# A hybrid encoder layer on one core: the first projection taken by halves of the rows for both column groups, with the input's halves loaded on ScalarE's queue

## The reference

```python
proj = x @ w_in
hq, hf, hi, hg, cq, ckv, su, lx, lg, gl = jnp.split(proj, IN_OFFSETS, axis=-1)
y_a = hgrn2_mixer(hq, hf, hi, hg, lb, hgrn_norm_w)
y_b = mla_mixer(cq, ckv, positions, ...)
y_c = s5_mixer(su, s5_a_re, s5_a_im, s5_log_dt, ...)
y_d = rglru_mixer(lx, lg, lru_conv_w, lru_conv_b, lru_wa, ...)
...
mix = jnp.sum(gates * branch_out, axis=2) @ w_out
h = layer_norm(DEEPNORM_ALPHA * x + mix, ln1_w, ln1_b)
ffn = moe_ffn(h, router_w, router_b, moe_w1, moe_b1, moe_w2, moe_b2)
return layer_norm(DEEPNORM_ALPHA * h + ffn, ln2_w, ln2_b)
```

```python
xc = lax.conv_general_dilated(x_raw, conv_w..., padding=[(LRU_CONV - 1, 0)], ...) + conv_b
r = jax.nn.sigmoid(jnp.einsum('bshi,hij->bshj', xb, wa)... + ba)
i = jax.nn.sigmoid(jnp.einsum('bshi,hij->bshj', xb, wx)... + bx)
```

## Time and profile before

| what | value |
|---|---|
| median of the timed runs | 1310.3 us (1309.55 to 1311.1) |
| the profiled execution's own time | 1309.58 us |
| its span | 1307.8 us |
| TensorE busy | 1251.4 us, 96% |
| VectorE / ScalarE busy | 455.6 us (35%) / 219.9 us (17%) |
| DMA, mean over the span | 351 GB/s, 458.99 MB |
| DMA, 460 to 1290 us | 428 to 431 GB/s |

### The profile page before, as it was taken

One profiled execution on the slowest core, in us unless ns is written; L12 is line 12 of the kernel. 1 busy time (PEld: TensorE's weight loads), 2 busy tenths in 40 slices (PEclk: granted clock), 3 DMA queues, 4 the chain that ended last, 5 costly groups with the idle time before them and its releaser, 6 DMA issues.

```text
span 1307.8 us, 15059 instructions
## 1 busy us (share of the span) xinstructions
PE 1251.4 (96%) x6094; PEld 637.9 (49%) x6094; DVE 455.6 (35%) x919; ACT 219.9 (17%) x430; POOL 4.0 (0%) x20
## 2 busy tenths in 40 slices
PE   9999999999999999999999999989999998999996
PEld 8888888998753333333333333333333333333331
DVE  4679965365347122121221212132121212132123
ACT  1432224131031101101011010101101010101102
POOL 0000000000000000000000000000000000000000
PEclk9999999999999999999999999999999999999998
DMA  9434344226788999999999999999999999999995
GB/s 366 164 144 142 113 146 161 99 95 229 277 346 363 396 432 431 432 431 432 432 431 428 431 430 431 432 430 430 429 429 430 430 431 432 432 432 426 426 424 237
DMA packets 29132, 458.99 MB, mean 351 GB/s; under 512 B 4464, under 2 KB 4848, under 8 KB 9104
## 3 DMA queue, kind: packets, MB, share of 16 engines
q1 hardware_dynamic: 25936, 454.04, 83.1%
q10 hardware_dynamic: 3136, 4.03, 0.9%
HBM read 457.02 MB, written 1.05 MB: 350 GB/s over the span
## 4 chain that ended last, share of the span: by engine, by line
PE 61%; DMA 22%; DVE 13%; ACT 2%; issue 1%; SPq 0%; DVEq 0%; ACTq 0%
DMA store<-in_moe_w 21%; PE banks L1208 16%; PE banks L1238 12%; PE banks L810 11%; PE banks L824 4%; PE banks L1214 3%; DVE store L1879 2%; PE banks L1090 2%; PE banks L1295 2%; PE banks L1140 2%; DVE store L1873 1%; DVE store L1876 1%; DVE store L1878 1%; ACT store L707 1%; PE banks L1224 1%
## 5 line engine op out<-in xcount | busy, mean ns | idle before, releaser
L1208 PE MATMUL banks<-store 128*64 128x512 f32 x1536 | 344.3, 597 | 23.5 <-DMA store<-in_moe_w 20.7
L1208 PEld LDWEIGHTS banks<-store 128*64 128x64 f32 x1536 | 111.0, 137 | 239.9 <-issue 210.4
L1238 PE MATMUL banks<-store 128*64 128x512 f32 x960 | 213.1, 596 | 0.0
L810 PE MATMUL banks<-store 128*128 128x256 f32 x896 | 196.4, 380 | 0.0
L810 PEld LDWEIGHTS banks<-store 128*128 128x128 f32 x896 | 169.5, 190 | 25.7 <-issue 3.0
L1873 DVE TENSOR_SCALAR store<-banks 128x512 f32<-128x512 f32 x32 | 22.1, 692 | 439.7 <-PE banks L1214 439.7
L1238 PEld LDWEIGHTS banks<-store 128*64 128x64 f32 x960 | 66.4, 137 | 145.4 <-issue 121.9
L1214 PE MATMUL banks<-store 128*64 128x512 f32 x512 | 116.9, 598 | 0.3 <-DMA store<-in_moe_w 0.3
L707 ACT ACTIVATE store<-store 128x512 f32<-128x512 f32 x30 | 19.0, 632 | 453.8 <-DVE store L1873 453.8
L1887 DVE COPY store<-banks 64x512 f32<-64x512 f32 x30 | 20.8, 694 | 206.8 <-PE banks L1238 206.8
L1140 PEld LDWEIGHTS banks<-store 128*128 128x128 f32 x480 | 57.0, 191 | 25.1 <-issue 23.5
(11 more groups left out here) (374 smaller groups left out, 837.9 us busy)
## 6 DMA issues: line engine op xcount, KB each, us to landing
store<-in_moe_w SPq DMA_DIRECT2D x78, 4096.0 KB, 35.3
store<-in_moe_w SPq DMA_DIRECT2D x32, 2048.0 KB, 16.1
store<-in_w_in SPq DMA_DIRECT2D x30, 1024.0 KB, 4.8
store<-in_w_branch SPq DMA_DIRECT2D x8, 1024.0 KB, 4.8
store<-in_moe_w SPq DMA_DIRECT2D x8, 1024.0 KB, 37.4
store<-in_w_out SPq DMA_DIRECT2D x4, 1024.0 KB, 6.8
store<-in_xT SPq DMA_DIRECT2D x2, 512.0 KB, 5.9
store<-in_w_in SPq DMA_DIRECT2D x2, 512.0 KB, 7.4
```

The costliest lines, as they stand in the source:

```text
L810: last = mm(b[:, j * SEQ:(j + 1) * SEQ], w[:, k, j * P:j * P + P], xT[:, k, :], start=k == 0, stop=k == KD - 1)
L1208: last = mm(bank[i][64 * ct:64 * ct + 64, :], xg[:, 2 * c + kk, col:col + CAP], w[:, kk, i * FF + ct * 512:i * FF + ct * 512 + 512], start ...
L1238: last = mm(bank[4][64 * dh:64 * dh + 64, :], actT[:, j, 64 * fh:64 * fh + 64], w[:, j, 512 * dh:512 * dh + 512], start=(fh, j) == (0, 0), ...
```

## The change

The two loads of `xT` move from SP to ScalarE, where they stand ahead of everything. SP keeps the two loads of the first chunk and goes straight on with the others. TensorE no longer finishes group 0 before group 1: it takes row blocks 0 to 3 for both groups when `first_in[0]` is full, then row blocks 4 to 7 for both groups when `first_in[1]` is. As both sums are then open at once, group 1 goes into bank 2 in place of the second half of bank 0. `warm_up(5)` is gone. ScalarE copies the two groups out by two instructions of 256 columns in place of one of 512. Nothing else is touched, and the number of matmuls of the projection is the same.

```diff
@@ sync
-            x_rows = A["xT"].rearrange("p (k t) -> p k t", k=KD)
             for i in range(pieces):
                 ks = slice(KD // pieces * i, KD // pieces * (i + 1))
-                sp.dma_start(xT[:, ks, :], x_rows[:, ks, :]).then_inc(first_in[i], 16)
                 sp.dma_start(first[:, ks, :], src[:, ks, :]).then_inc(first_in[i], 16)
@@ scalar
+            x_rows = A["xT"].rearrange("p (k t) -> p k t", k=KD)
+            for i in range(pieces):
+                ks = slice(KD // pieces * i, KD // pieces * (i + 1))
+                act.dma_start(xT[:, ks, :], x_rows[:, ks, :]).then_inc(first_in[i], 16)
             act.wait_ge(first_in[0], 32)
             act.dma_start(vec[:, :], A["vec"]).then_inc(S["vec_in"], 16)
@@
-            for i in range(2):
-                b = projected(("lx", i))
-                nc.scalar.activation(lx[:, 2 * i:2 * i + 2, 3:3 + SEQ], b[:, :].rearrange("p (a b) -> p a b", a=2), ACT.Copy)\
-                    .then_inc(S["proj_evac"], 1)
+            first_halves = (projected(("lx", 0)), bank[2])
+            nc.scalar.activation(lx[:, 0, 3:3 + SEQ], first_halves[0][:, 0:SEQ], ACT.Copy)
+            nc.scalar.activation(lx[:, 1, 3:3 + SEQ], first_halves[1][:, 0:SEQ], ACT.Copy).then_inc(S["proj_evac"], 1)
+            b = projected(("lx", 1))
+            nc.scalar.activation(lx[:, 2:4, 3:3 + SEQ], b[:, :].rearrange("p (a b) -> p a b", a=2), ACT.Copy).then_inc(S["proj_evac"], 1)
@@ tensor
-            for j in range(2):
-                for k in range(KD):
-                    if j == 0 and k == KD // pieces:
-                        warm_up(5)
-                    if j == 0 and k % (KD // pieces) == 0:
-                        pe.wait_ge(first_in[k // (KD // pieces)], 32)
-                    last = mm(bank[0][:, j * SEQ:(j + 1) * SEQ], w[:, k, j * P:j * P + P], xT[:, k, :], start=k == 0, stop=k == KD - 1)
+            for i in range(pieces):
+                pe.wait_ge(first_in[i], 32)
+                for j in range(2):
+                    for k in range(KD // pieces * i, KD // pieces * (i + 1)):
+                        last = mm(bank[2 * j][:, 0:SEQ], w[:, k, j * P:j * P + P], xT[:, k, :], start=k == 0, stop=k == KD - 1)
```

## The result

The changed kernel takes 1313.53 us (median of 12 runs, 1312.89 to 1318.94); the kernel before, run on the same chip, takes 1311.07 us (12 runs, 1309.43 to 1314.21). The ratio is 1.0017 [1.0009, 1.0025]: slower by 2.5 us between the medians. That is less than the 0.2% which the prediction took for the least change that can be told from none, though the interval lies above 1, and it is outside the predicted range of 1307.4 to 1312.0. The profiled execution took 1314.56 us, its span is 1312.8. The profile of before was 1.5 us under the median of these 12 runs, so of the 5.0 us between the two spans not all is the change's.

The account below looks back on a forecast made before the run. The prediction took the weights' transfers to pace the end and `vec`'s landing to decide the start. TensorE 0, copies 0 and `vec` -1.0 took the 1310.3 us median to 1309.3 us, range 1307.4 to 1312.0.

Parts of the forecast that it names:

- the clock, costed at nothing: First projection: clock stayed at 2.4 GHz across 1.74 us idle; that idleness stays, the later one shrinks, so cost 0.
- `vec` 1.0 us earlier: Start of VectorE's chain: the load of `vec` lands at 14.2 us, gaining 1.0 us, out of 0 to 3.0.
- the edit can neither lengthen nor shorten the stream: Weights' stream to the end: a microsecond gained or lost before 315 us moves the end by the same microsecond.
- TensorE's part: First projection: no gap, ending 1.3 to 1.6 us earlier, at 14.3 to 14.7, all waited away at the gates.
- on the path this is worth nothing: TensorE's faster first projection only makes the wait ahead of the gates 3.1 to 3.4 us instead of 1.8; gain 0.
- Copies: ScalarE's two copies of 256 columns cost at most 0.58 us more, covered by the wait for `lx 1`; taken as 0.
- nothing moves: Rival on the load of `vec`: it lands at 15.2 us as before, time 1310.2 us; chance 0.22.
- at most 0.44 us: First loads: if a second issuing engine saves only issue time, the whole edit gains at most this, giving 1309.9 us.
- My line through the sizes of two other transfers: Lower bound for `vec`: from loads of 256 and 512 KB, its 65 KB take 2.0 us, landing at 11.9 to 13.0.

Follow-up runs that it names:

- e11: The changed kernel run again with nothing altered: 1314.02 us, 1.0026 of the kernel before.
- e15: The changed kernel run a third time with nothing altered: 1313.41 us, 1.0020 of the kernel before.
- e2: The kernel before with only the two `xT` loads moved to ScalarE: 1311.73 us, 1.0001 of the kernel before.
- e6: The kernel before with `warm_up(6)` for `warm_up(11)` at its start, five products of ones fewer: 1312.32 us, 1.0003 of the kernel before.
- e12: The kernel before with VectorE's convolutions 2 and 3 moved ahead of the S5 spreading: 1310.67 us, 0.9995 of the kernel before.
- e3: The changed kernel with both `xT` loads back on SP, ahead of the chunk's halves: 1312.79 us, 1.0012 of the kernel before.
- e5: The changed kernel with `warm_up(16)` for `warm_up(11)` at its start, five products of ones more: 1313.73 us, 1.0010 of the kernel before.
- e13: The changed kernel with `warm_up(16)` and six products of ones ahead of later waits, gates' wait left open: 1313.07 us, 1.0017 of the kernel before.
- e1: The changed kernel with 9 and 2 products of ones filling TensorE's waits ahead of the third and fourth gate products: 1312.17 us, 1.0002 of the kernel before.
- e14: The same kernel as e1, run again: 1312.28 us, 1.0012 of the kernel before.
- e8: The kernel of e1 with `warm_up(16)` for `warm_up(11)` at its start: 1312.06 us, 1.0002 of the kernel before.
- e16: The kernel of e7 with all four first loads on SP again: 1307.35 us, 0.9966 of the kernel before.
- e7: The changed kernel with VectorE's convolutions 2 and 3 right behind 0 and 1, and `warm_up(16)` for `warm_up(11)`: 1308.93 us, 0.9980 of the kernel before.

## Why the prediction was wrong, step by step

Three steps failed: the clock, costed at nothing; `vec` 1.0 us earlier; and "the edit can neither lengthen nor shorten the stream". They stand below among those that held.

- **TensorE's part: right on its own place.** Projection without a gap, end at 14.74 (14.3 to 14.7 said), all of it waited away ahead of the gates (2.7 us; "2 us or more"). That "on the path this is worth nothing" was right for the gain, and wrong as a whole: see the clock. In e11 and e15 the projection ended at 16.3, the low clock having taken 1.7 us, and the gates waited 1.3 us.
- **"I cost the clock at nothing": wrong.** I looked at the idle time at the start and not at the wait that the same sentence made longer. It was followed by 3.5 us at 1.2 GHz in the profile of the result: 0.9 us. It did not come in e11 and e15; there the stretch was at 8.6 us, behind the very idle time that I had called harmless from one profile. What came in all three is a stretch further on: one at 1.2 GHz that begins at 381 to 386 us stands in all 14 profiles with TensorE's changed order, and in none of the 4 with the old one (before, e2, e6, e12), and those 14 lose 2.0 to 5.1 us between 65 and 110 MB against the profile before, those three 1.6 to 2.0. By the table of low stretches the one near 385 us is worth 0.8 us in e11 and e15 and 2.2 in the profile of the result.
- **Copies: right.** Two of 0.37 and 0.38 us at 19.69 and 19.95, under the wait for `lx 1`. Free.
- **`vec` 1.0 us earlier: a mis-sized term, measured 0.03.** It was issued 0.12 us earlier, not 0.3, and took 7.51 us, not less. The rival that fits is "nothing moves": the 7.4 us are not set by what stands ahead of it in its own queue, since with half of `xT` there (e2 7.4, changed 7.5) and with nothing there (e6 7.5) they are the same. Only e3 (7.1) and e5 (6.9) were shorter. Of the Trainium skill (Trainium Kernel Development and Optimization, Key Constraints) I had said that by its rule the edit of the loads is worth at most 0.44 us: e2 fits, with 1.0001 [0.9992, 1.0011], but an interval of 1.2 us either way can't tell 0.44 us from nothing. My line through the sizes of two other transfers was no estimate of a small one.
- **"The edit can neither lengthen nor shorten the stream": wrong, and the step that I had not taken at all.** The stream itself kept its rate; what I had left out is where its last transfers land. I priced `warm_up(5)` by its time alone, which is nothing, since it lay in a wait. It is also ten matmul records of code. Without them the fetches of code near 692 us are three, not two, one packet more goes through the weights' engines, and the last wait is 1.15 us longer. The three profiles of the changed kernel lose 1.20, 1.19 and 1.06 us behind 457 MB; the kernel before with five products fewer loses 1.25.

So between 1309.3 and 1313.53 lie 4.2 us: 0.8 is this chip's before against the runs that I had (1311.07 and 1310.3), 1.0 the gain of `vec` that did not come, and 2.5 the loss. Of the loss the profiles show 1.2 at the tail, as a property of the shorter program; in the times of e5 and e13 the padding alone gave nothing that they can resolve (each 0.2 or 0.3 us from the changed kernel, e5 above it on another chip, e13 below e15 on its own), so as a part of the median it is argued, not shown. Filled wait and length together gave back 1.8 (e1) and 1.1 (e14). The rest lies between 65 and 110 MB, where the changed kernel's three profiles have the stretch near 385 us and before, e2, e6 and e12 have none. From e6, the old order with the same short program, to e11 and e15 the end moves by 0.8 and 1.15 us, and the stretch near 385 us costs 0.8 in both.

**Open.** Why the changed order goes with the low clock near 385 us: TensorE's waits from 360 to 395 us are no longer than before (0.6 us in sum, and 1.1), what it multiplies there is the same, and no run here took it away alone. It stayed when the length was changed (e5, e13) and when the gates' wait was filled (e1, e8, e14), so how filling gains its microsecond is not shown. And e16 beats e7 by 1.6 us, from another batch. Their profiles end 2.5 us apart, of which the low clock accounts for 2.2: near 382 us e7's stretch is 6.8 us long and costs 3.1, e16's is 3.4 us long and costs 0.9. Whether the loads have a part in that is not shown.

## What to carry to other kernels

An engine made faster ahead of a wait that another engine ends gains nothing, and can lose by the clock (here at 40 us once in three profiles, and near 425 us in ten of ten with the longer wait); first take away the wait (here three lines moved on VectorE), then both gains come (e16). In a kernel whose end runs at the rate of the transfers, instructions that cost no time still cost code: after removing some, compare the packets of code and the last waits for weights before blaming the edit's own place. And when a profile of before is one execution, set it beside the median of its runs, and take more than one: 1.5 us of the 5 us seen here were never the change's. Beside each profile list where the clock was low; executions of one kernel differ by that.

## What the hardware showed that I had not expected

- Products of ones removed in the first 6 us move a wait at 1283 us from 0.27 to 1.63 us (before and e6), with one packet of 16 KB of code more on the way.
- A packet of code takes 1.07 us; the last of 16 engines steps 1.1 to 1.4 us away every eighth packet, and in a stream without pauses the lateness adds up: the spread of a transfer's landings grows from 1.8 to 8.0 us between 480 and 1285 us.
- A low clock ahead of a wait cost nothing here, and the same wait without it had a low clock behind it: near 425 us TensorE waited 2.3 us in ten profiles, and each time 3.4 us at 1.2 GHz followed and cost 1.7; in the eight with 0 to 0.76 us none followed.
- A load of 65 KB took 6.9 to 7.5 us from its issue beside SP's chunks, behind half of `xT` in its queue or behind nothing; and issued ahead of that half, it made the half 2.7 us later (13.2 in place of 10.5), far more than the time of its own bytes (0.15 us at the 428 GB/s of the earlier trace rows).
